# A two-block transformer kernel: constant products ahead of the first slab, a new order for the first head round, branch splits over the last gate slabs, and a few reordered steps

## The chip, the cores and the metric

The kernel runs on one core of one Trainium2 chip. The metric is the device time of one execution in microseconds (us). A core has TensorE (PE, matrix products into PSUM banks), VectorE (DVE), ScalarE (ACT), GpSimd (POOL) and SyncE (SP, which here issues nearly all DMAs). The engines run their own instruction streams in order and meet through semaphores.

## The reference

Two blocks work on x of 512 tokens by 1024 features, all in float32.

```python
# block 1: gated delta rule (8 heads, chunks) and forgetting attention (8 heads)
u = rmsnorm(x, norm_mix_g);  proj = u @ w_in          # q, k, v, z, gates, fq, fk, fv, ff, gate_a, gate_b
qkv = silu(causal_depthwise_conv([gq, gk, gv]))       # then l2norm of q and k, per head
o_a = gated_delta_rule(q, k, v, g, beta);  o_b = forgetting_attention(fq, fk, fv, log_f)
merged = sigmoid(gate_a) * (o_a @ w_proj_gdn) + sigmoid(gate_b) * (o_b @ w_proj_fox)
h = x + merged @ w_out;  x = h + square(relu(rmsnorm(h) @ w_up)) @ w_down
# block 2: retention (4 heads) and sliding-window attention with sinks (16 query, 2 key heads)
ry = silu(rg) * head_group_norm(retention(rotary(rq), rotary(rk), rv));  ay = window_attention(...)
merged = sigmoid(gate_a) * (ry @ w_ret_out) + sigmoid(gate_b) * (ay @ w_attn_out)
x = x + merged @ w_out;  x = x + (silu(h2 @ w_gate) * (h2 @ w_up)) @ w_down
return rmsnorm(x, lnf_g)
```

## The kernel before, in words

**Slabs.** All large weights are cut into 302 slabs of 1024 by 128 (8 tiles of 128x128). SP loads a slab into one of four `slab_raw` buffers. ACT casts it to `slab_hi` (L269), POOL subtracts to get `slab_lo` (L276, two halves), and only then may SP load the slab four places later into that buffer. An activation is split in the same way: ACT writes `u_hi` (L492), DVE writes `u_lo` (L497). One slab is then 24 products on PE: hi by hi (L287), hi by lo activation (L288) and lo by hi (L289) for each of 8 tiles, all into one PSUM bank. PE waits for `slab_lo` before the first product of a slab. DVE takes the finished bank away ("evacuation", eJ for slab J) and multiplies it by the norm row `r_row`.

**Orders.** Every engine walks the same list of tokens. `sJ.T` is tile T of slab J (on ACT and POOL `sJ.0` is the split of slab J+2), `eJ` is the evacuation, and every other token is a step that each engine takes part in or ignores. For block 1, `FIRST` orders head round 0 (7 slabs, and the gate and norm setup `nsq`, `nrow`, `nrc`, `gates0` to `gates4`), `ORDER` the rounds 1 to 7, in which the small steps of the head before are spread between the slabs of the next, and `LAST`, built from `ORDER`, the eight gate slabs ahead. `cvX.W` are the convolution steps on DVE, `thX`/`slX` the tanh on ACT and the silu on DVE, `tq`, `tfq`, `tk`, `tfk` transposes of q and k on PE. `YL` and `XL` are the two products of a level of the triangular inverse (L1518): Y on PE, a copy on ACT, X on PE, then a subtraction and a transpose on DVE, on which the next Y waits. In block 2 `FIRST2`, `ORDER2` and `LAST2` do the same for 10 key/value and first-head slabs, three rounds of 8 slabs and 8 gate slabs. There `sp0` to `sp2` build the retention states on DVE (L1198) from products on PE, `ro` (L937, L939) reads them, `M2` is the scaling of attention probabilities on DVE (L1257 to L1264), `T2`/`T3` transposes of probabilities (L977), `sg` and `bn` DVE steps.

**Start.** SP issues the gains, half of x (1 MB), slab 0, the other half, slab 1, four small tables, `x_tok` (2 MB, for the norm), slabs 2 and 3. One semaphore, `ld_small`, covers the small tables and `x_tok`. PE begins when `slab_lo` of slab 0 is there.

**Between rounds and merge.** After the gate slabs, the outputs of both branches are split (`branch_hi` on ACT L564, `branch_lo` on DVE L577, 16 pairs of tiles each engine). In block 1 these steps are already spread over the last gate slabs (`brK` in `LAST`); in block 2 they all come after the last gate slab.

**End.** The last norm adds squares of 8 tiles (ACT, POOL). PE sums over partitions with a matrix of ones (L517, L519), DVE scales (L533), POOL takes the power (L508), PE spreads it to a row (L525), DVE multiplies the 8 output tiles (L1388), and SP stores each.

Of the kernel before, what the change touches and what calls it, by code (L numbers as in the profile page):

```python
# [26 lines left out]
P = 128  # L27
T = 512
NT = T // P
# [105 lines left out]
def program(nc, dram, out):  # L135
# [23 lines left out]
    with ExitStack() as ctx:  # L159
# [120 lines left out]
        def slab_products(pe, ph, i, j, bank, x_hi, x_lo, ks=range(KT), n_k=KT):  # L280
# [9 lines left out]
            if ks[-1] == n_k - 1:  # L290
# [78 lines left out]
                   s1.1 bs tv T0 bi s1.2 s1.3 S1 s1.4 vp E1 s1.5 s1.6 kpd s1.7 P1 s2.0 Y3 s2.1 s2.2 X3 O0 e1 s2.3  # L369
# [34 lines left out]
        FIRST = [t for t in ORDER if is_slab(t) or is_evac(t) or t in LATE]  # L404
        FIRST.remove("tq")
        FIRST.insert(FIRST.index("tfq"), "tq")
        FIRST.insert(FIRST.index("s0.0") + 1, "nsq")
        FIRST.insert(FIRST.index("s2.3"), "nrow")
        FIRST.insert(FIRST.index("e0"), "nrc")
        FIRST.insert(FIRST.index("s1.2"), "gates0")  # L410
        FIRST.insert(FIRST.index("s1.7"), "gates0t")
        FIRST.insert(FIRST.index("e1") + 1, "gates1")
        FIRST.insert(FIRST.index("e3") + 1, "gates2")
        FIRST.insert(FIRST.index("e4") + 1, "gates3")
        FIRST.insert(FIRST.index("s6.0") + 1, "gates4")
# [94 lines left out]
        def norm_pe(pe, n):  # L510

            pe.wait_ge(sem("norm_sum"), (n - 1) * (KT - 1) + (KT - 2 if n == 4 else KT - 1))
            if n == 4:
                pe.wait_ge(sem("norm_sq"), n * KT + 1)
            for t in range(NT):
                q = slice(t * P, (t + 1) * P)
# [3 lines left out]
            mm.then_inc(sem("norm_ps"), 1)  # L520

        def norm_pe_row(pe, n):
            pe.wait_ge(sem("norm_pool"), n + 1)
            for t in range(NT):
                mm = pe.transpose(bF[:, t * P:(t + 1) * P], r_col[:, t:t + 1].to_broadcast([P, P]), ident[:])  # L525
            mm.then_inc(sem("norm_ps"), 1)

        def norm_dve(dve, n):
            if n == 0:
                dve.wait_ge(sem("norm_sq"), 1)  # L530
            else:
                dve.wait_ge(sem("norm_ps"), 2 * n)
            dve.tensor_scalar(ms_col[:], ms_col[:] if n == 0 else bF[:, 0:NT], 1.0 / D, EPS, ALU.mult, ALU.add)\  # L533
                .then_inc(sem("norm_ms"), 1)
# [254 lines left out]
        def mlp_dve(dve):  # L789
            def part(i):  # L790
                for j in range(16):
# [67 lines left out]
                    s3.0 e2 sp0 lg3 s3.1 s3.2 sp1 E3 s3.3 s3.4 M2 sp2 s3.5 s3.6 s3.7 ro tg M3 s4.0 T2 e3 s4.1 bn  # L859
                    s4.2 T3 sg s4.3 s4.4 s4.5 O1 nm s4.6 s4.7 ev1 s5.0 ty s5.1 s5.2 yo s5.3 e4 s5.4 swan rbn s5.5 s5.6  # L860
# [11 lines left out]
        for tok, place in zip(("rbn", "swqn", "swkn", "rqn", "rkn", "swan", "ran"),  # L872
                              ("s5.6", "s6.2", "s6.4", "s6.6", "s7.2", "s8.2", "s8.6")):
# [15 lines left out]
        def ret_pe(pe, tiles, transposes):  # L889
            def per_round(tokens, ph, i, c):  # L890
# [59 lines left out]
                def logits(a_):  # L950
# [7 lines left out]
                    pe.sem_inc(sem("logits_begun"), 1)  # L958
# [23 lines left out]
                def outs(a_):  # L982
# [5 lines left out]
                    pe.sem_inc(sem("outs_begun"), 1)  # L988
# [18 lines left out]
        def ret_act(act):  # L1007
# [7 lines left out]
            def per_round(tokens, ph, i, c):  # L1015
# [66 lines left out]
                def ev(a_):  # L1082
# [5 lines left out]
                          "swkn": lambda: swrn(1), "swa1": swa1, "swan": swan}  # L1088
                for a_ in range(2):
                    stages[f"ev{a_}"] = lambda a_=a_: ev(a_)  # L1090
# [8 lines left out]
        def ret_dve(dve, step):  # L1099
# [17 lines left out]
            def per_round(tokens, ph, i, c):  # L1117
# [154 lines left out]
                for u in range(4):  # L1272
                    stages[f"lg{u}"] = lambda u=u: logits(u)
                    stages[f"M{u}"] = lambda u=u: sums(u)
                if c is None:
# [25 lines left out]

        FFN_PARTS = [(ph_ffn, 0, 8), (ph_ffn, 1, 8), (ph_ffn_end, 0, FF2_TILES - 16)]
# [33 lines left out]
        def ffn_act(act):  # L1336
# [19 lines left out]
            square(KT - 1)  # L1356

        def ffn_dve(dve):
# [28 lines left out]
            for m in range(KT):  # L1387
# [3 lines left out]
        def ffn_pool(pool):  # L1391
# [6 lines left out]
            norm_pool_scale(pool, 4)  # L1398

# [27 lines left out]
        def after_heads_dve(dve, step):  # L1427
# [4 lines left out]
            for k in range(KT):  # L1432
                branch_lo(dve, 1, k)
# [900 lines left out]
```

## Time and profile before

| | us |
|---|---|
| three runs | 1964.81, 1964.97, 1965.12 |
| profiled execution, its own time | 1964.55 |
| its span, first to last instruction | 1962.8 |
| PE busy | 1918.7 |
| DVE, POOL, ACT busy | 939.1, 914.5, 686.3 |

Times inside the trace count from the start of the span, and 1.75 us lie around it. A PE row of a product is longer than the distance to the next one, because products overlap in the array; what a product costs is the distance between starts.

### The profile page before, as it was taken

To read this page: it belongs to the slowest core of one execution; us is meant where nothing else is said; L and a number is where in the kernel's file an instruction comes from. 1 tells how busy PE (TensorE), PEld (TensorE's weight loads), DVE (VectorE), ACT (ScalarE), POOL (GpSimd) and SP (SyncE) were. 2 spreads that over 40 slices of the span, in tenths; PEclk is the share of its full clock that TensorE was granted. 3 is DMA by queue.
4 is the path that set the end of the run, shared out by engine and by line. 5 is a ranking of instruction groups with operands and counts; after the bars stand their busy time and mean duration, and the time that the engine had idled before them with its cause. 6 is when DMAs were issued, how large, how long until landed. Compare 5 with 4: busy or idle time off the path is not lost.

```text
span 1962.8 us, 27161 instructions
## 1 busy us (share of the span) xinstructions
PE 1918.7 (98%) x9893; PEld 1569.9 (80%) x9893; DVE 939.1 (48%) x1642; ACT 686.3 (35%) x1379; POOL 914.5 (47%) x695
## 2 busy tenths in 40 slices
PE   7899999999999999999999999999999999999997
PEld 5788878888788888888888877778788888888886
DVE  4777777777652222121212467778522235244143
ACT  4344333443332234232324445545422332222122
POOL 3444345443444465444445533434345556555455
PEclk9999999999999999999999999999999999999999
DMA  5122111221223342333332322112133323323232
GB/s 195 56 86 85 64 64 43 85 85 64 65 77 106 129 143 97 97 97 97 96 97 97 118 76 75 64 64 65 64 141 104 100 86 97 108 86 101 92 97 75
DMA packets 53046, 178.55 MB, mean 91 GB/s; under 512 B 6704, under 2 KB 7664, under 8 KB 52720
## 3 DMA queue, kind: packets, MB, share of 16 engines
q1 hardware_dynamic: 52480, 174.95, 27.1%
q10 hardware_dynamic: 496, 2.65, 0.4%
q8 instruction: 46, 0.75, 0.2%
q14 instruction: 24, 0.20, 0.0%
HBM read 173.35 MB, written 4.23 MB: 90 GB/s over the span
## 4 chain that ended last, share of the span: by engine, by line
PE 88%; DVE 8%; ACT 2%; issue 2%; DMA 0%; POOL 0%; DVEq 0%; POOLq 0%; ACTq 0%; SPq 0%
PE bank L287 26%; PE bank L289 25%; PE bank L288 25%; PE bank L1507 2%; PE bank L1501 2%; PE bank L1518 1%; PE bank L1697 1%; PE bank L1684 1%; PE bank L992 1%; DVE att_neg_max L1251 1%; ACT slab_hi L269 1%; PE bank L963 1%; PE bank L977 0%; DVE block_rows L2076 0%; PE bank L937 0%
## 5 line engine op out<-in xcount | busy, mean ns | idle before, releaser
L276 POOL TENSOR_TENSOR slab_lo<-slab_raw,slab_hi 128x512 fp32r<-128x512 f32 x604 | 818.2, 1380 | 954.8 <-ACT slab_hi L269 954.7
L287 PE MATMUL bank<-u_hi,slab_hi 128*128 128x512 f32 x1584 | 653.8, 413 | 14.1 <-POOL slab_lo L276 13.5
L289 PE MATMUL bank<-u_hi,slab_lo 128*128 128x512 f32 x1584 | 620.3, 392 | 0.0
L288 PE MATMUL bank<-u_lo,slab_hi 128*128 128x512 f32 x1584 | 618.6, 391 | 0.0
L269 ACT CAST slab_hi<-slab_raw 128x1024 fp32r<-128x1024 f32 x302 | 313.9, 1045 | 219.6 <-PE bank L289 218.5
L287 PEld LDWEIGHTS bank<-u_hi,slab_hi 128*128 128x128 f32 x1584 | 298.6, 189 | 76.4 <-issue 18.2
L289 PEld LDWEIGHTS bank<-u_hi,slab_lo 128*128 128x128 f32 x1584 | 297.9, 188 | 64.1
L288 PEld LDWEIGHTS bank<-u_lo,slab_hi 128*128 128x128 f32 x1584 | 299.1, 189 | 55.2 <-issue 1.9
L287 PE MATMUL bank<-hidden_hi,slab_hi 128*128 128x512 f32 x432 | 168.4, 390 | 0.3
L288 PE MATMUL bank<-hidden_lo,slab_hi 128*128 128x512 f32 x432 | 168.1, 389 | 0.0
L289 PE MATMUL bank<-hidden_hi,slab_lo 128*128 128x512 f32 x432 | 168.1, 389 | 0.0
L503 DVE TENSOR_TENSOR residual<-residual,bank 128x512 f32<-128x512 f32 x48 | 33.0, 688 | 200.6 <-PE bank L289 200.6
L287 PEld LDWEIGHTS bank<-hidden_hi,slab_hi 128*128 128x128 f32 x432 | 81.1, 188 | 18.4 <-DVE residual L1383 1.6
L288 PEld LDWEIGHTS bank<-hidden_lo,slab_hi 128*128 128x128 f32 x432 | 81.1, 188 | 16.8
L289 PEld LDWEIGHTS bank<-hidden_hi,slab_lo 128*128 128x128 f32 x432 | 81.1, 188 | 16.7
L670 DVE SCALAR_TENSOR_TENSOR mtmp<-mtmp,bank 128x512 f32<-128x512 f32 x32 | 22.0, 688 | 129.9 <-PE bank L289 129.7
L1348 ACT ACTIVATE tmp<-tmp 128x512 f32<-128x512 f32 x22 | 13.9, 633 | 176.6 <-DVE tmp L1369 176.6
L801 DVE SCALAR_TENSOR_TENSOR tmp<-bank,r_row 128x512 f32<-128x512 f32 x32 | 22.1, 692 | 85.0 <-PE bank L289 84.9
L1383 DVE TENSOR_TENSOR residual<-residual,bank 128x512 f32<-128x512 f32 x24 | 16.5, 688 | 94.8 <-PE bank L289 94.8
L772 ACT ACTIVATE tmp<-tmp 128x512 f32<-128x512 f32 x32 | 20.2, 632 | 109.0 <-DVE tmp L801 109.0
L486 POOL TENSOR_TENSOR sq_sum<-sq_sum,mtmp 128x512 f32<-128x512 f32 x27 | 35.0, 1298 | 47.4 <-ACT mtmp L477 47.4
L287 PE MATMUL bank<-branch_a_hi,slab_hi 128*128 128x512 f32 x128 | 51.4, 401 | 3.0 <-DVE branch_a_lo L577 3.0
(353 smaller groups left out, 2581.0 us busy)
## 6 DMA issues: line engine op xcount, KB each, us to landing
slab_raw<-slabs SPq DMA_DIRECT2D x302, 512.0 KB, 3.5
g_and_cum_rows<-row_store SPq DMA_DIRECT2D x7, 512.0 KB, 6.4
residual<-x_t SPq DMA_DIRECT2D x2, 1024.0 KB, 7.0
x_tok<-x SPq DMA_DIRECT2D x1, 2048.0 KB, 12.9
residual<-x_t SPq DMA_DIRECT2D x1, 2048.0 KB, 9.1
residual_store<-residual SPq DMA_DIRECT2D x1, 2048.0 KB, 9.8
residual<-residual_store ACTq DMA_DIRECT2D x1, 2048.0 KB, 9.1
out_t<-residual SPq DMA_DIRECT2D x8, 256.0 KB, 2.1
```

What stands on the lines that cost most here:

```text
L269: act.copy(w_hi[s][:], raw[s][:]).then_inc(s_hi, 1)
L276: ins = pool.tensor_tensor(w_lo[s][:, ks, :], raw[s][:, ks, :], w_hi[s][:, ks, :].bitcast(F32), ALU.subtract)
L287: pe.matmul(bank, w_hi[s][:, k, :], x_hi[:, k, :], start=first, stop=False)
L288: pe.matmul(bank, w_hi[s][:, k, :], x_lo[:, k, :], start=False, stop=False)
L289: mm = pe.matmul(bank, w_lo[s][:, k, :], x_hi[:, k, :], start=False, stop=last)
L486: pool.tensor_tensor(sq_sum[:], sq_sum[:], mtmp[m % 2][:], ALU.add).then_inc(sem("norm_sum"), 1)
L503: ins = dve.tensor_tensor(h_res[:, m, :], h_res[:, m, :], bank[:], ALU.add)
L670: dve.scalar_tensor_tensor(out=merge_g[j][:], in0=merge_g[j][:], scalar=1.0, in1=branch_banks(m, ahead)[j][:], op0=ALU.add, op1=ALU.mult). ...
L772: act.activation(tmp[2 + t % 2][:], tmp[t % 2][:], ACT.Square).then_inc(sem("hid_sq"), 1)
L801: dve.scalar_tensor_tensor(out=tmp[j % 2][:], in0=bank_slab[j % 2][:], scalar=0.0, in1=r_row[:], op0=ALU.max, op1=ALU.mult).then_inc(sem(" ...
L1501: mm = pe.matmul(out_[:, c], lhs[:, c], rhs[:, c], start=start, stop=stop)
L1507: mm = pe.transpose(out_[:, c], in_[:, c], ident[:])
```

## The change

Seven parts:

1. **Constant products.** PE begins with 34 products of the constant matrix `ones` with itself (128x128, f32) into a bank that nothing reads, as soon as DVE has set `ones`.
2. **Loads.** x comes in three pieces (2, 2 and 4 tiles), slab 0 right behind the first, then slabs 1 and 2 and the small tables, `x_tok` under a semaphore of its own, then slab 3.
3. **First two slabs.** DVE instead of POOL makes `slab_lo` of slab 0, between `u_lo` tiles 1 and 2. POOL waits until all of `u_lo` is done. PE takes slab 0 by an explicit list, high parts first, and of slab 1 first all products with `slab_hi`, then the eight with `slab_lo`.
4. **Order of round 0.** `FIRST` is written out: evacuations and convolutions start earlier relative to the slabs, and the second half of `gates1` becomes `gates1b`.
5. **Orders.** `X3` moves behind `O0 e1 s2.3`; in block 2 `sp2` before `M2`, `sg` and `s4.3` before `T3`, `kva` from s2.4 to s2.7, `swan` and `ran` from slab 8 to slab 7.
6. **Branch splits.** In block 2 `br0` to `br7` go into `LAST2`, from s5.4 to s7.3.
7. **Last norm.** PE sums the seven added tiles into one bank early and the last tile alone into another; tiles 6 and 7 are scaled on ACT in advance and multiplied by the row on POOL, DVE keeps six.

Some semaphores are merged or renamed. The core of the diff:

```diff
-s1.1 bs tv T0 bi s1.2 ... s2.1 s2.2 X3 O0 e1 s2.3
+s1.1 bs tv T0 bi s1.2 ... s2.1 s2.2 O0 e1 s2.3 X3
...
-        FIRST = [t for t in ORDER if is_slab(t) or is_evac(t) or t in LATE]
...
+        FIRST = """s0.0 nsq s0.1 s0.2 s0.3 s0.4 s0.5 s0.6 s0.7 s1.0 nrc s1.1 gates0 s1.2 s1.3 s1.4 s1.5 s1.6 s1.7 s2.0
+                   nrow e0 s2.1 cv0.0 gates0t s2.2 cv0.1 s2.3 cv0.2 s2.4 cv0.3 s2.5 e1 th0 s2.6 gates1 s2.7 cv1.0 s3.0
+                   cv1.1 s3.1 e2 s3.2 sl0 s3.3 gates1b s3.4 cv1.2 s3.5 cv1.3 s3.6 tq s3.7 th1 s4.0 s4.1 gates2 s4.2 e3
+                   s4.3 cv2.0 s4.4 cv2.1 s4.5 cv2.2 s4.6 cv2.3 gates3 s4.7 tfq sl1 th2 s5.0 s5.1 e4 s5.2 sl2 s5.3 gates4
+                   s5.4 tk s5.5 s5.6 tfk s5.7 s6.0 e5 s6.1 cola s6.2 colh s6.3 s6.4 s6.5 s6.6 s6.7""".split()
...
-                mm = pe.matmul(bF[:, t:t + 1], sq_sum[:, q], ones[:, 0:1], start=True, stop=n != 4)
-                if n == 4:
-                    mm = pe.matmul(bF[:, t:t + 1], mtmp[1][:, q], ones[:, 0:1], start=False, stop=True)
+            if n == 4:
+                pe.wait_ge(sem("norm_sq"), n * KT + 1)
+                for t in range(NT):
+                    mm = pe.matmul(bE[:, t:t + 1], mtmp[1][:, t * P:(t + 1) * P], ones[:, 0:1], start=True, stop=True)
...
-            if rnd == 1:
-                for k in range(KT):
-                    branch_hi(act, 1, k)
...
-                    s3.0 e2 sp0 lg3 s3.1 s3.2 sp1 E3 s3.3 s3.4 M2 sp2 s3.5 s3.6 s3.7 ro tg M3 s4.0 T2 e3 s4.1 bn
-                    s4.2 T3 sg s4.3 s4.4 s4.5 O1 nm
+                    s3.0 e2 sp0 lg3 s3.1 s3.2 sp1 E3 s3.3 s3.4 sp2 M2 s3.5 s3.6 s3.7 ro tg M3 s4.0 T2 e3 s4.1 bn
+                    s4.2 sg s4.3 T3 s4.4 s4.5 O1 nm
...
+        for k, place in enumerate(("s5.4", "s5.6", "s6.0", "s6.2", "s6.4", "s6.6", "s7.1", "s7.3")):
+            LAST2.insert(LAST2.index(place), f"br{k}")
...
-        FIRST2.insert(FIRST2.index("s2.4"), "kva")
+        FIRST2.insert(FIRST2.index("s2.7"), "kva")
...
-                              ("s5.6", "s6.2", "s6.4", "s6.6", "s7.2", "s8.2", "s8.6")):
+                              ("s5.6", "s6.2", "s6.4", "s6.6", "s7.2", "s7.3", "s7.7")):
...
+        POOL_TILES, DVE_TILES = (6, 7), (0, 1, 2, 3, 4, 5)
...
+            for m in POOL_TILES:
+                act.activation(h_res[:, m, :], h_res[:, m, :], ACT.Copy, scale=gains[:, 4, m:m + 1])
+            act.wait_ge(sem("norm_ps"), 11)
+            act.copy(r_row[:], bE[:]).then_inc(sem("act_step"), 1)
...
+            for m in POOL_TILES:
+                pool.tensor_tensor(h_res[:, m, :], h_res[:, m, :], r_row[:], ALU.mult).then_inc(sem("pool_result"), 1)
...
-            for k in range(KT):
-                branch_lo(dve, 1, k)
...
+        WARM = 34
+        FIRST_SLAB = [[("hh", 0)], [("hh", 1), ("hl", 0)], [("hl", 1), ("hh", 2)],
+                      [("hh", 3), ("lh", 0), ("lh", 1), ("lh", 2), ("lh", 3)],
+                      [("hl", 2), ("hl", 3), ("hh", 4)], [("hh", 5), ("lh", 4), ("lh", 5), ("hl", 4)],
+                      [("hl", 5), ("hh", 6)], [("hh", 7), ("lh", 6), ("lh", 7), ("hl", 6), ("hl", 7)]]
+        X_PIECES = ((0, 2, "ld_x_first"), (2, 4, "ld_x_second"), (4, 8, "ld_x"))
...
+            for m in (0, 1, 2, 3, 6, 4, 5, 7):
...
+            def second_slab(t, bank):
+                if t == 0:
+                    pe.wait_ge(s_hi, 2)
+                pe.matmul(bank[:], w_hi[1][:, t, :], u_hi[:, t, :], start=t == 0, stop=False)
+                pe.matmul(bank[:], w_hi[1][:, t, :], u_lo[:, t, :], start=False, stop=False)
+                if t == KT - 1:
+                    pe.wait_ge(s_lo, 2)
+                    for k in range(KT):
+                        mm = pe.matmul(bank[:], w_lo[1][:, k, :], u_hi[:, k, :], start=False, stop=k == KT - 1)
+                    mm.then_inc(s_used, 1)
+
+            pe.wait_ge(sem("setup_dve"), 1)
+            for n in range(WARM):
+                pe.matmul(bA[:, 0:P], ones[:], ones[:], start=True, stop=True)
...
+                if k == 1:
+                    dve.wait_ge(s_hi, 1)
+                    dve.tensor_tensor(w_lo[0][:], raw[0][:], w_hi[0][:].bitcast(F32), ALU.subtract).then_inc(s_lo, 1)
...
-            for j in range(LEAD):
-                split_lo(pool, ph_heads, 0, j)
+            pool.wait_ge(s_lo, 1)
+            pool.wait_ge(sem("u_lo"), KT)
+            split_lo(pool, ph_heads, 0, 1)
```

## Rows read from the trace of the kernel before

**Rows 1.** The page, part 1: busy time (share of the span), instructions.
```profile
PE 1918.7 (98%) x9893; PEld 1569.9 (80%) x9893; DVE 939.1 (48%) x1642; ACT 686.3 (35%) x1379; POOL 914.5 (47%) x695
```
**Rows 2.** Waits of PE, whole span: who waited for whom: us, times, longest.
```profile
PE bank L287 <- POOL slab_lo L276: 13.5, 1, 13.5
PE bank L937 <- DVE ret_state L1198: 5.5, 4, 1.4
PE bank L287 <- DVE branch_a_lo L577: 3.0, 2, 2.7
PE bank L1518 <- ACT inv_and_prod L1813: 2.8, 8, 0.6
PE bank L1507 <- DVE ck L1983: 2.0, 1, 2.0
PE bank L1507 <- DVE cq L1983: 1.7, 1, 1.7
...
PE bank L977 <- ACT att_probs_t L1079: 0.9, 4, 0.3
PE bank L1507 <- DVE raw_fq L1904: 0.7, 1, 0.7
PE bank L963 <- DVE att_q L1115: 0.6, 1, 0.6
PE bank L1507 <- DVE ret_k L1150: 0.5, 1, 0.5
```
**Rows 3.** Timeline of the start: start us, us, what, xcount [idle before <-releaser].
```profile
1.11 0.27 DVE L1877 MEMSET inv_t_full<- 64x256 f32 x1
...
6.69 1.28 ACT L492 ACT_TABLE_LOAD   x1 [6.69 <-DMA residual<-x_t]
...
8.74 1.41 DVE L497 SCALAR_TENSOR_TENSOR u_lo<-residual,gains,u_hi 128x512 fp32r<-128x512 f32 x2 [7.35 <-ACT u_hi L492]
...
10.16 3.78 ACT L492 ACTIVATE u_hi<-residual,gains 128x512 fp32r<-128x512 f32 x6
...
10.91 7.68 DVE L497 SCALAR_TENSOR_TENSOR u_lo<-residual,gains,u_hi 128x512 fp32r<-128x512 f32 x6 [0.76 <-ACT u_hi L492]
```
**Rows 4.** Chain that ended last, 13 to 75 us: start us, us, what.
```profile
18.52 0.43 PE bank L289
...
19.51 0.23 PE bank L289
...
69.07 0.44 PE bank L1507 x4
...
72.73 0.89 PE bank L1501 x8
```
**Rows 5.** Windows: PE, PEld, DVE, ACT, POOL busy, granted clock, DMA share, GB/s.
```profile
4.00:6.00 2.00, 0.00 (x0) 0.00 (x0) 0.00 (x0) 0.00 (x0) 0.00 (x0) 1.00 1.04 404
```
**Rows 6.** Timeline of head round 2, the step X3 on DVE, then Y4 on PE.
```profile
150.03 0.45 DVE L2095 STREAM_TRANSPOSE inv_and_prod<-inv_t 128x256 f32<-128x256 f32 x1
...
151.86 0.68 PE L1518 MATMUL bank<-inv_and_prod,a_levels 64*64 64x64 f32 x16
```
**Rows 7.** Window in the branch splits of block 2 (columns as in rows 5).
```profile
1410.00:1411.00 1.00, 1.00 (x4) 0.81 (x3) 1.00 (x3) 1.00 (x3) 0.00 (x0) 0.50 0.00 0
```
**Rows 8.** Chain that ended last, 1405 to 1418 us.
```profile
1405.92 0.24 PE bank L289
...
1408.83 0.60 DVE branch_b_lo L577
...
1417.31 0.50 PE bank L287
```
**Rows 9.** Timeline of the end.
```profile
1950.79 0.35 PE L517 MATMUL bank<-ones,sq_sum 128*128 128x1 f32 x2 [1.53 <-ACT mtmp L477]
...
1952.75 0.16 DVE L533 TENSOR_SCALAR ms_col<-bank 128x4 f32<-128x4 f32 x1 [2.76 <-PE bank L519]
...
1954.95 5.36 DVE L1388 SCALAR_TENSOR_TENSOR residual<-residual,gains,bank 128x512 f32<-128x512 f32 x8 [2.04 <-PE bank L525]
```

More of the change, by code:

```diff
@@ L1274, in per_round @@
                     stages[f"M{u}"] = lambda u=u: sums(u)
+                for k in range(KT):
+                    stages[f"br{k}"] = lambda k=k: branch_lo(dve, 1, k)
                 if c is None:
@@ L1386, in ffn_dve @@
             dve.wait_ge(sem("norm_ps"), 9)
-            for m in range(KT):
+            dve.scalar_tensor_tensor(out=ms_col[:], in0=bE[:, 0:NT], scalar=1.0 / D, in1=ms_col[:], op0=ALU.mult,
+                                     op1=ALU.add).then_inc(sem("norm_ms"), 1)
+            dve.wait_ge(sem("norm_ps"), 10)
+            for m in DVE_TILES:
                 dve.scalar_tensor_tensor(out=h_res[:, m, :], in0=h_res[:, m, :], scalar=gains[:, 4, m:m + 1],
@@ L1452, in _ @@
                 sp.dma_start(dst, src).then_inc(sem(name), 16)
-            sp.dma_start(x_tok[:], dram["x"].rearrange("(n p) d -> p n d", p=P)).then_inc(sem("ld_small"), 16)
-            for j in range(2, ph_heads.n):
+            sp.dma_start(x_tok[:], dram["x"].rearrange("(n p) d -> p n d", p=P)).then_inc(sem("ld_x_tok"), 16)
+            first_slab(3)
+            for j in range(SLOTS, ph_heads.n):
                 s = ph_heads.slot(j)
@@ L1519, in quads, with first_slab @@
                 return mm
+            def first_slab(t, bank):
+                for kind, k in FIRST_SLAB[t]:
+                    first, last = (kind, k) == ("hh", 0), (kind, k) == ("hl", KT - 1)
+                    if kind == "hh":
+                        if k == 0:
+                            pe.wait_ge(s_hi, 1)
+                        pe.wait_ge(sem("u_hi"), k + 1)
+                        mm = pe.matmul(bank[:], w_hi[0][:, k, :], u_hi[:, k, :], start=first, stop=False)
+                    elif kind == "hl":
+                        pe.wait_ge(sem("u_lo"), k + 1)
+                        mm = pe.matmul(bank[:], w_hi[0][:, k, :], u_lo[:, k, :], start=False, stop=last)
+                    else:
+                        if k == 0:
+                            pe.wait_ge(s_lo, 1)
+                        mm = pe.matmul(bank[:], w_lo[0][:, k, :], u_hi[:, k, :], start=False, stop=False)
+                mm_last = mm
+                if t == KT - 1:
+                    mm_last.then_inc(s_used, 1)
+            def second_slab(t, bank):
[3 more added lines that the diff above has]
+                pe.matmul(bank[:], w_hi[1][:, t, :], u_lo[:, t, :], start=False, stop=False)
+                if t == KT - 1:
+                    pe.wait_ge(s_lo, 2)
+                    for k in range(KT):
+                        mm = pe.matmul(bank[:], w_lo[1][:, k, :], u_hi[:, k, :], start=False, stop=k == KT - 1)
[3 more added lines that the diff above has]
+                pe.matmul(bA[:, 0:P], ones[:], ones[:], start=True, stop=True)
             def head_round(tokens, i, c):
@@ L1533, in slab @@
                     if isinstance(i, int) and i == 0 and j == 0:
[L1534 removed]
+                        first_slab(t, bank)
+                        return
+                    if isinstance(i, int) and i == 0 and j == 1:
+                        second_slab(t, bank)
+                        return
                     slab_products(pe, ph, ph_i, j, bank[:], u_hi, u_lo, ks=(t,))
```

104 lines of the change are left out of this document (54 added, 50 removed).

## The prediction

> **What bounds the kernel now.** I began with the page. TensorE is busy for 98% of the span [rows 1], so no other engine can be the bound as a whole, and the change takes no products away (it adds some). What is left to win is time in which TensorE does nothing or runs at the lower clock, and that is found in two views: the list of waits with TensorE as the waiting engine [rows 2], and the timeline at the few places that this list names. The reader is to see in [rows 2] that one wait, 13.5 us at the very start, is nearly half of the sum, and that the rest is small waits that come back once a round. The list leaves one kind of loss out: products that run but slowly. It shows in the distance between starts. The last product of the slow stretch at the start takes 0.43 us to the next, one of the fast stretch 0.23 [rows 4]; that is 1.2 against 2.4 GHz for 512 columns. The column of the granted clock does not show it at the start (it reads 1.00 there), while it reads 0.50 in the second slow stretch, in the branch splits of block 2 [rows 7].
>
> **Part 1 to 4, the start, by sums.** Before, TensorE starts at 13.5 us, when POOL has finished the low part of slab 0, and runs 13 products at the low clock, until 18.9. The first step of round 1 starts at 69.07 [rows 4]. The 55.6 us between hold 13 x 0.20 = 2.6 us of low clock and 2.0 + 1.7 + 0.7 = 4.4 us of waits for the convolved q and k and for an evacuation [rows 2]. So the work of round 0 itself is 55.6 - 2.6 - 4.4 = 48.6 us, and the new start of round 1 is the time at which real products begin, plus 48.6, plus new waits.
>
> When do real products begin? DVE has set the constants at 1.4 us [rows 3], and then come 34 products in f32 of 128 columns. Four such products stand in the trace as 8 instructions in 0.89 us [rows 4], so one instruction costs 0.111 us at full clock and 34 products are 68 of them. No row has this shape at the low clock; between 0.111 (the weight load hidden) and twice that, I take 0.222, because the 512-column products do double. The low clock lasted 5.4 us after the idle start. So 5.4 / 0.222 = 24 instructions at the low clock, 44 x 0.111 = 4.9 us at the full one, and the end is 1.4 + 5.4 + 4.9 = 11.7 us. If the clock rose at once it would be 1.4 + 68 x 0.111 = 9.0; if not at all during these products, 1.4 + 68 x 0.222 = 16.5.
>
> Are the data there at 11.7? The first MB of x had landed at 6.7 [rows 3]; at 404 GB/s [rows 5] half a MB less is 1.3 us less, 5.4. ACT loads its table (1.28), makes two tiles of `u_hi` at 0.63, which is what six of them in 3.78 us cost [rows 3], and casts slab 0 (1024 columns, an estimate of 1.1 from the same row): 9.1. DVE then makes `slab_lo` of slab 0; no row has DVE at 1024 columns, so it lies between one split of 512 columns, 0.6 [rows 8], and two with a start-up, 1.4; I take 1.3, since twice the columns are what it does: 10.4. After that come six tiles of `u_lo`. Before they took 7.68 us, 1.28 each, while POOL was splitting slabs; the first two, with POOL idle, took 1.41 together [rows 3]. POOL now waits until they are done, so I count 0.67 each, 4.0, and the last one stands at 14.4 us. ACT's last `u_hi` does not set it: six more at 0.63 from 9.1 and the rest of x, another 1.5 MB at 404 GB/s behind slab 0, end near 13.1. TensorE, from 11.7, reaches the last low activation as its 24th product, at 11.7 + 23 x 0.227 = 16.9, so nothing waits, and the margin is 2.5 us. Slab 1 asks for its high part at 17.1 (ready near 14) and its low part only after gates0 (24 products, 5.5 us) and the other high products, near 26; POOL makes it from 14.4 to 17.3. The delay of POOL costs nothing for that reason.
>
> What is late next is the setup of the norm. `x_tok` goes ahead of slab 3 only, so it is the sixth MB; five more at 404 GB/s behind the first are 12.4 us, with the small tables near 20. Four squares on ACT of 1024 columns (an estimate, 1.1 each) and the power on POOL, and r is there near 26. `nrow` stands at 11.7 + 17.5 = 29.2 on TensorE. From there DVE has a chain: row, e0, four steps of q's convolution, e1, six small gate steps, and so on. Written out at 0.7 us a step it gives silu of q at 38.4 (TensorE wants it at 39), the gate table at 41.2 (wanted at 41.6), e3 at 45.9 (wanted at 46.6), silu of k at 49.4 (wanted at 50.4). Each margin is positive and under 1.2 us, so I take no new wait, and up to 2 us for the range. The second half of the gate steps needs two table loads on ACT, and between the two halves DVE now works at convolutions. Sum: 11.7 + 48.6 = 60.3 against 69.07, a gain of **8.8 us**.
>
> **Part 5, orders.** `X3` waits 2.8 us in 8 rounds for a copy on ACT that is queued behind the cast of a slab [rows 2]. Behind `O0` and one tile of a slab (0.2 + 0.7 us) the copy is long done: gain 2.8. The price can be on the next step: before, DVE ends the transpose for `Y4` at 150.48 and `Y4` starts at 151.86 [rows 6], 1.4 us of room; X3 runs 0.6 us later net of the wait, and e1 on DVE, which it lets pass, uses the wait, so 0.4 or more is left. I count nothing. In block 2, `ro` waits 5.5 us in four rounds for the last state [rows 2]. DVE writes that state behind the four operations of `M2`, and the releaser named in the row is this write. With `sp2` ahead of `M2` it comes before TensorE wants it; its product stands three tiles earlier (2.0 us). `M2` moves back by one short operation, which `T2` does not feel, as it stands behind all 14 instructions of `ro`. Gain 5.5, and if only half of the wait were `M2`, 2.8. `T3` waited 0.9 in all for copies on ACT and gets one more tile, 0.7 us each: gain 0.9. `kva` three tiles later clears 0.5, and `swan` and `ran` a slab earlier clear 0.6 at the first logits [rows 2]. ACT then waits for the evacuation of slab 6 with the swaps, and behind it are only casts which wait for slab 8 anyway. Sum: **10.3 us**.
>
> **Part 6, branch splits.** The last gate product ends at 1406.16 in the chain, the product on the last low tile of branch a starts at 1417.31 [rows 8] and the slab ends with it, 3 products later, at 1418.3. Unhindered it would end 24 x 0.227 = 5.4 after 1406.0, at 1411.4. So 6.9 us hang on the splits: 2.7 in the wait, the rest in the low clock [rows 7] and in splits of DVE at 0.60 each, two for each tile [rows 8]. After the change DVE has, from s5.4 to the end of slab 7 (20 tiles, 13.6 us), 16 x 0.60 = 9.6 us of splits and two evacuations of 1.2: 12.0. They fit, and TensorE is hindered only if e5 is late for slab 7, which begins 5.4 before 1406.0, at 1400.6. Ahead of e5 stand br0 to br2, 3.6 us from about 1393.8, so e5 ends near 1398.6. What is queued behind the splits on ACT is the cast of slab 8: it waits for six copies, ends near 1397.5, and POOL has the low part at 1400 for a use at 1406. SP's load of slab 12 waits for that low part, and is wanted 20 us later. Gain **6.9 us**.
>
> POOL works at two slabs meanwhile. The rows show that this matters: `u_lo` at 1.28 us beside POOL and 0.7 without [rows 3], the splits at 0.60 beside an idle POOL [rows 8]. The page "SBUF — State Buffer" of the Trainium skill (section Who interferes with whom) says that a VectorE instruction with two SBUF inputs and a GpSimd one that reads SBUF exclude each other for the whole instruction; [rows 3] agrees. By that rule these two slabs block DVE for another 5.1 us, the last split comes at 1411 instead of 1406, and the gain is 6.4 instead of 6.9.
>
> **Part 7, the end.** 16 instructions at 0.11 us lie between the last square and DVE's scaling at 1952.75 [rows 9]. Eight of them move ahead of the last square: 0.9. DVE's 8 tiles at 0.67 [rows 9] become 6: 1.3. POOL's two begin behind four more instructions on PE and a copy on ACT (1.1 us) and have until DVE's sixth, so POOL may take 1.4 us a tile where DVE takes 0.67; I take it that they just end. Stores go out one by one, of 256 KB, 0.65 us each at the rate of [rows 5], and that takes back 0.1. Gain **2.1 us**.
>
> **Sum.** 8.8 + 10.3 + 6.9 + 2.1 = 28.1 us. The profiled execution took 1964.55, so 1936.45; the median of the runs is 0.4 above it, and I predict **1936.8 us**.
>
> **Rivals.** (A) The forecast.
> (B) *The clock does not rise during the constant products*, because they load weights as long as they multiply. Real products begin at 16.5 and the first 13 run at the low clock: 4.8 + 2.6 = 7.4 us less gain, 1944.2. For it: no row of this shape starts from the low clock. Against: rounds with many small products stay at 0.23.
> (C) *Small waits come back elsewhere.* The gains of part 5 and of the conv chain leave margins of 0.3 to 1 us. If half of part 5 is lost at the next step (5.2 us), 1942.0. For it: DVE, the second busiest engine [rows 1], makes nearly all that these steps wait for. Against: each of these waits had nothing of the same kind behind it in [rows 2].
> (D) *The splits move the wait to slab 7*, which doesn't do what it says. If the six splits ahead of e5 run at 1.28 instead of 0.60, e5 ends 4.1 us later, 2.2 after slab 7 wants it: 1939.0.
> (E) *Slower: the low clock stays.* If the constant products and then round 0 itself run at the low clock, each us of work costs one more. Real products begin at 16.5 (4.8 later), and the gain of 28.1 is used up when 23 of the 48.6 us of round 0 have run at half speed; with all of it, 1936.8 + 4.8 + 48.6 = 1990. Against: the low stretch at the start ended after 5.4 us of steady work, though of products of another shape.
>
> **Chances.** A 0.64, B 0.09, C 0.12, D 0.04, E 0.03 (0.01 of it stopping within 0.2% of before), and 0.08 for a larger gain than A: the gaps that TensorE's queue leaves around each cleared wait, and constant products that end at 9 to 10, together up to 4 us, 1932.8. Range 1932.8 to 1942.0: the low end is that case, the high end is C, and it leaves out B and E, 0.12. Less than 0.2% either way, 3.9 us, is about what a measurement of this kernel can't tell from no change; only E and an error of over 20 us reach it. So faster 0.97 (all but E), same 0.01, slower 0.02.
>
> **What would show it.** In the changed trace: real products from 11.7 us at 0.23 apart; the last `u_lo` near 14.4; the first step of round 1 near 60; no wait of TensorE for the copy before X3 nor for the state; the first merge product right behind the last gate product, with the clock at 1.00; DVE's last output tile 2.2 us sooner after the last square. The prediction is wrong if constant products last to 16, if round 0 has waits of over 2 us for DVE, or if a wait appears at slab 7 of the last gate round.

## The result, and the profile after

The changed kernel takes **1939.64 us** (median of four runs, 1939.38 to 1940.0), against 1964.89 for the kernel before in the same comparison; the ratio is 0.9875, 95% interval [0.9864, 0.9887]. The forecast was 1936.8 with a range of 1932.8 to 1942.0. The profiled execution took 1939.53, with a span of 1937.7; its own gain in span is 1962.8 - 1937.7 = 25.1 us, where the sum of the terms said 28.1.

The page after, part 1, answers to [rows 1]:

```profile
PE 1920.6 (99%) x9965; PEld 1576.2 (81%) x9965; DVE 949.7 (49%) x1642; ACT 688.3 (36%) x1382; POOL 917.7 (47%) x695
```

The waits of TensorE after answer to [rows 2] (who waited for whom: us, times, longest):

```profile
PE bank L1757 <- DVE k_dec L2110: 3.1, 8, 1.3
PE bank L1575 <- DVE inv_t_full L1937: 1.4, 1, 1.4
PE bank L519 <- POOL r_col L501: 1.4, 1, 1.4
PE bank L287 <- DVE branch_a_lo L573: 1.2, 1, 1.2
PE bank L1529 <- DVE raw_fq L1967: 0.9, 1, 0.9
...
PE bank L1633 <- DVE table L2007: 0.5, 1, 0.5
```

The wait of 13.5 us for `slab_lo` is gone, and so are those for `ret_state`, for the convolved q and k, and for the copy at `X3`. The first line was 0.2 us in one place before. What it has gained is almost exactly the wait of 2.8 us at `X3` that went. L1757 is `O0`, the step that `X3` was moved behind.

**Where the 25.1 us came from.** The same step stands in both traces, so the difference of its start times tells how much had been gained by then. Read at the borders of the stages it gives:

| stage | forecast | measured |
|---|---|---|
| start, to the first step of round 1 | 8.8 | 8.6 |
| rounds of block 1 (`X3`) | 2.8 | -0.3 |
| to the rounds of block 2 (`kva`, `swan`, `ran`) | 1.1 | 1.9 |
| four rounds of block 2 (`sp2`, `T3`) | 6.4 | 8.5 |
| merge of block 2 (splits) | 6.9 | 5.3 |
| last norm and stores | 2.1 | 1.2 |
| sum | 28.1 | 25.1 (rounded terms: 25.2) |

The sum is off by 3.0, with errors of both signs in it: 2.9 us too little in the rounds of block 2 and on the way to them, 5.8 us too much elsewhere. That the total came so near is in part luck.

The start. The chain of the changed kernel, start us and us (`x68` are the constant products):

```profile
1.43 9.36 PE bank L1575 x68
10.79 0.46 PE bank L1550 x2
...
28.61 0.70 DVE r_row L534
...
46.06 1.13 DVE block_rows L2029
47.21 0.70 DVE raw_fq L1967
47.96 0.66 PE bank L1529 x4
...
60.49 0.44 PE bank L1529 x4
```

Real products begin at 10.8 instead of the forecast 11.7, and round 1 at 60.49 against 69.07 in [rows 4]. Between the two the chain leaves TensorE and runs over DVE, with two table loads of ACT (1.28 us each) in it, from the row of the norm at 28.6 to `raw_fq`.

The merge. The timeline of DVE ahead of it (start us, us, what):

```profile
1387.81 0.68 DVE L1144 TENSOR_TENSOR residual<-bank,r_row 128x512 f32<-128x512 f32 x1
1388.52 0.80 DVE L1146 TENSOR_SCALAR residual<-residual,round_bias 128x512 f32<-128x512 f32 x1
1389.25 1.77 DVE L573 TENSOR_TENSOR branch_a_lo<-branch_a,branch_a_hi 128x512 fp32r<-128x512 f32 x1
1390.95 1.77 DVE L573 TENSOR_TENSOR branch_b_lo<-branch_b,branch_b_hi 128x512 fp32r<-128x512 f32 x1
1392.65 0.68 DVE L573 TENSOR_TENSOR branch_a_lo<-branch_a,branch_a_hi 128x512 fp32r<-128x512 f32 x1
1393.25 0.68 DVE L573 TENSOR_TENSOR branch_b_lo<-branch_b,branch_b_hi 128x512 fp32r<-128x512 f32 x1
```

A split takes 1.77 us or 0.68. POOL's low parts of slabs run from 1382.4 to 1392.2 with a pause of 0.27 us, and every split that starts in that stretch is a long one. TensorE takes the last tile of branch a at 1393.38, after a wait of 1.15 us.

The end. The timeline of the last norm answers to [rows 9]:

```profile
1926.79 1.05 PE L512 MATMUL bank<-ones,mtmp 128*128 128x1 f32 x8 [0.66 <-ACT mtmp L470]
1927.95 0.16 DVE L1390 SCALAR_TENSOR_TENSOR ms_col<-bank,ms_col 128x4 f32<-128x4 f32 x1 [1.62 <-PE bank L512]
...
1930.00 4.04 DVE L1394 SCALAR_TENSOR_TENSOR residual<-residual,gains,bank 128x512 f32<-128x512 f32 x6 [1.89 <-PE bank L519]
...
1931.51 2.49 POOL L1407 TENSOR_TENSOR residual<-residual,r_row 128x512 f32<-128x512 f32 x2 [2.31 <-ACT r_row L1359]
```

DVE ends at 1934.04, 1.3 us sooner after its first tile than before, as forecast; but the span ends at 1937.7. From DVE's first tile to the end it was 7.85 us before (1954.95 to 1962.8) and is 7.7 now.

### The profile page after: what moved, and what is told of

Its sections match the earlier page's. It is cut to its first block, busy times and chain, and to the rows that moved or that the text cites. A ratio compares the mean times of both kernels' runs of the same rounds, so it can differ in the third digit from the quotient of the medians.

```text
span 1937.7 us, 27308 instructions
## 1 busy us (share of the span) xinstructions
PE 1920.6 (99%) x9965; PEld 1576.2 (81%) x9965; DVE 949.7 (49%) x1642; ACT 688.3 (36%) x1382; POOL 917.7 (47%) x695
## 4 chain that ended last, share of the span: by engine, by line
PE 92%; DVE 6%; issue 1%; ACT 0%; DVEq 0%; POOL 0%
PE bank L287 27%; PE bank L289 26%; PE bank L288 26%; PE bank L1529 2%; PE bank L1523 2%; PE bank L1540 1%; PE bank L1757 1%; PE bank L1744 1%; PE bank L986 1%; PE bank L957 1%; PE bank L971 1%; PE bank L1575 0%; DVE block_rows L2147 0%; DVE branch_a_lo L573 0%; DVE branch_b_lo L573 0%
## 5 line engine op out<-in xcount | busy, mean ns | idle before, releaser
L287 PE MATMUL bank<-u_hi,slab_hi 128*128 128x512 f32 x1568 | 646.3, 412 | 0.2
L289 PE MATMUL bank<-u_hi,slab_lo 128*128 128x512 f32 x1568 | 613.0, 391 | 0.0
L288 PE MATMUL bank<-u_lo,slab_hi 128*128 128x512 f32 x1568 | 611.5, 390 | 0.0
L1347 ACT ACTIVATE tmp<-tmp 128x512 f32<-128x512 f32 x22 | 13.9, 632 | 176.6 <-DVE tmp L1372 176.6
L479 POOL TENSOR_TENSOR sq_sum<-sq_sum,mtmp 128x512 f32<-128x512 f32 x27 | 35.1, 1299 | 47.4 <-ACT mtmp L470 47.4
L485 ACT ACTIVATE u_hi<-residual,gains 128x512 fp32r<-128x512 f32 x32 | 22.7, 723 | 89.8 <-DVE residual L496 85.0
```

Source lines behind the costliest of these rows:

```text
L287: pe.matmul(bank, w_hi[s][:, k, :], x_hi[:, k, :], start=first, stop=False)
L288: pe.matmul(bank, w_hi[s][:, k, :], x_lo[:, k, :], start=False, stop=False)
L289: mm = pe.matmul(bank, w_lo[s][:, k, :], x_hi[:, k, :], start=False, stop=last)
L479: pool.tensor_tensor(sq_sum[:], sq_sum[:], mtmp[m % 2][:], ALU.add).then_inc(sem("norm_sum"), 1)
L485: act.activation(u_hi[:, m, :], h_res[:, m, :], ACT.Copy, scale=gains[:, n, m:m + 1])\
```

## The experiments

Each edits the changed kernel; an edit not shown is told in its expectation. All times are medians of four runs. They come from several comparisons, and the kernel before, run beside each, had medians from 1963.26 to 1964.89 us. So a difference of about 1.5 us or less between medians of two comparisons shows little by itself, and what is said of such gains rests on the distances in the traces.

**1. Where `X3`'s gain went.** Two kernels, `X3` back in its old place, and `O0` one tile later:

```diff
-s2.1 s2.2 O0 e1 s2.3 X3
+s2.1 s2.2 X3 O0 e1 s2.3     (a2)
+s2.1 s2.2 s2.3 O0 e1 X3     (a1)
```

> The changed kernel with X3 back in its old place (X3 O0 e1 s2.3). Theory 1, the move exchanged one wait for another of the same size: the wait for ACT's copy at X3 (2.8 us) returns, the wait at O0 (3.1 us) goes, and the time is 1939.6 within 0.7 us. Theory 2, the prediction's sum: the move gains 2.8 us and something else ate the rest, so without it the time is 1942.4.

Measured: **1939.33 us**, the changed kernel's time. The waits of TensorE with `X3` back:

```profile
PE bank L1540 <- ACT inv_and_prod L1873: 2.5, 8, 0.4
```

The wait for `k_dec` is not in its list. The move by itself is worth nothing.

> The changed kernel, with O0 one slab tile later (s2.3 O0 e1 X3 for O0 e1 s2.3 X3), so that X3 stays where the change put it. Theory 1, the wait only moved: in the changed kernel TensorE waits 3.1 us in 8 rounds at O0 for DVE's k_dec, each wait 0.25 to 0.4 us, and the tile of 0.68 us covers them; each listed wait costs some 0.15 us more than its row says, so the time falls from 1939.6 by 3 to 4.5 us, to 1935 to 1936.6. Theory 2, DVE's chain behind X3 (subtraction, transpose, then Y4) has no room left: the wait comes up at Y4 or T1 instead, and the time stays within 1 us of 1939.6.

Measured: **1936.59 us** (1935.77 to 1937.83), 3 us faster than the changed kernel. From 80 to 500 us TensorE has no wait in the list at all, where the changed kernel has this:

```profile
PE bank L1757 <- DVE k_dec L2110: 1.5, 6, 0.3
```

Each round is 0.51 us shorter, for 0.25 of listed wait; the other 0.26 stands beside it. Only the last head keeps some:

```profile
PE bank L1757 <- DVE k_dec L2110: 0.6, 1, 0.6
PE bank L1529 <- DVE probs L2227: 0.4, 1, 0.4
```

So the room behind `X3` that the forecast doubted was there (Y4 waits for nothing), and the step that failed was one it never looked at: `O0`, which took `X3`'s place in the order. In round 2 of the changed kernel TensorE could begin `O0` at 139.13, DVE's `k_dec`, for which it waits, ends at 139.40, and `O0` begins at 139.55.

**2. The merge: DVE beside POOL.**

> The changed kernel with the branch splits of block 2 behind the last gate slab again, on ACT and DVE, as before the change. By the distances between the two traces the move gained 5.3 us, so 1944.9; the prediction's term was 6.9, so 1946.5 by that; if the extra work that the splits bring to DVE and POOL in the gate round costs elsewhere, less than 5 us.

Measured: **1944.96 us**, 5.3 more than the changed kernel. The term is 5.3, not 6.9. The distances in the traces give 5.3 against this kernel and against the kernel before alike, although TensorE's clock is low for 3.4 us of the splits here and for 6.8 there. DVE makes a pair of splits in 1.20 us, and TensorE takes a tile in 0.7 us at the full clock and 1.28 at the low one. When the clock rises it catches up, and in both kernels it takes the last tile of branch a 0.05 or 0.06 us after DVE has made it. So the splits set the pace, and the low clock, to which the prediction gave a part of the price, cost nothing here.

> The changed kernel with nearly all of POOL's work during the last gate round of block 2 left out: of each of the eight low parts made in that round (slabs 2 to 9 counted from its start) only 16 columns of one tile are computed. Theory 1, DVE's branch splits take 1.77 us each where POOL subtracts at the same time and 0.6 to 0.7 where it does not: all 16 now take 0.6 to 0.7, DVE is done some 8 us earlier, the wait before the last tile of branch a goes, and the time falls by 1.3 to 1.6 us to 1938.0 to 1938.3. Theory 2, the long splits have another cause (ACT's writes, DMAs): they stay at 1.77 us and the time stays at 1939.6.

```diff
+            if ph is ph_gates2:
+                pool.tensor_tensor(w_lo[s][:, 0, 0:16], raw[s][:, 0, 0:16], w_hi[s][:, 0, 0:16].bitcast(F32),
+                                   ALU.subtract).then_inc(s_lo, 1)
+                return
```

Measured: **1938.16 us**, 1.5 less. Groups of DVE from 1374 to 1394 us by form (busy us, mean ns), first the changed kernel, then this one:

```profile
L573 DVE TENSOR_TENSOR branch_a_lo<-branch_a,branch_a_hi 128x512 fp32r<-128x512 f32 x8 | 8.8, 1095 | 0.7 <-ACT branch_a_hi L560 0.7
L573 DVE TENSOR_TENSOR branch_b_lo<-branch_b,branch_b_hi 128x512 fp32r<-128x512 f32 x8 | 8.7, 1093 | 0.0
```

```profile
L577 DVE TENSOR_TENSOR branch_b_lo<-branch_b,branch_b_hi 128x512 fp32r<-128x512 f32 x8 | 6.6, 821 | 0.0
L577 DVE TENSOR_TENSOR branch_a_lo<-branch_a,branch_a_hi 128x512 fp32r<-128x512 f32 x8 | 5.5, 684 | 0.7 <-ACT branch_a_hi L564 0.7
```

All eight splits of branch a now take 0.68 us; of branch b only the last, which falls beside the slabs that POOL still does in full, is long. The wait at the merge is gone (1.5 us there by the distances), and POOL is shown as the cause. The page "SBUF — State Buffer" of the Trainium skill (section Who interferes with whom) says that a VectorE instruction with two SBUF inputs contends with a GpSimd instruction that reads SBUF. This case agrees, at 1.77 against 0.68 us.

> The changed kernel with the evacuation e6 of the last gate round behind the last branch split br7 (three tiles later), so that DVE makes the splits 1.5 us earlier. Theory 1, DVE is short of time before the merge because its splits take 1.77 us beside POOL: each us given back there counts, and of the 1.6 us that TensorE loses at the last tile of branch a 1.2 to 1.6 come back: 1938.0 to 1938.4. Theory 2, DVE would then run its next instructions more often against POOL's and gain nothing: 1939.6 within 0.4.

Measured: **1939.41 us**, no gain in the time, as theory 2 had it; by the distances in the trace 0.4 us come back at the merge, where theory 1 put 1.2 to 1.6. DVE ahead of the merge in this kernel:

```profile
1387.97 1.78 DVE L573 TENSOR_TENSOR branch_a_lo<-branch_a,branch_a_hi 128x512 fp32r<-128x512 f32 x1
1389.67 1.77 DVE L573 TENSOR_TENSOR branch_b_lo<-branch_b,branch_b_hi 128x512 fp32r<-128x512 f32 x1
1391.36 1.77 DVE L573 TENSOR_TENSOR branch_a_lo<-branch_a,branch_a_hi 128x512 fp32r<-128x512 f32 x1
```

The evacuation e6 costs 0.68 and 0.80 us beside a busy POOL, and 0.68 and 0.49 alone. Taken out of POOL's time, it makes room for one more split, which POOL stretches to 1.77. Time given back to DVE is worth little as long as POOL holds it to one split per 1.7 us.

> The changed kernel with another order of the branch splits on ACT and DVE, in both blocks: all eight tiles of branch a first, then the eight of branch b (before: a0, b0, a1, b1 and so on). The merge takes a's eight tiles in its first 5.4 us and b's in the next 5.4. Theory 1, the wait at the merge comes from the order only, since b's tiles are made before they are needed: a's last tile stands some 6 us earlier, b's last one stays at 1393.9 and is wanted at about 1396.5, so the wait of 1.2 us and some 0.3 beside it go: 1938.0 to 1938.4. Theory 2: DVE as a whole is too late for the merge, and the wait moves to branch b or to the evacuation e7: 1939.6 within 0.4.

```diff
-            for hi, br in ((a_hi, br_a), (b_hi, br_b)):
-                act.copy(hi[:, k, :], br[:, k, :]).then_inc(sem("br_hi"), 1)
+            hi, br = ((a_hi, br_a), (b_hi, br_b))[k // 4]
+            for q in (2 * k % KT, 2 * k % KT + 1):
+                act.copy(hi[:, q, :], br[:, q, :]).then_inc(sem("br_hi"), 1)
```

(`branch_lo` and TensorE's counts follow in the same way.) Measured: **1938.65 us** (1937.88 to 1938.92), 1.0 less by the medians and 1.4 at the merge by the distances in the trace. DVE in this kernel:

```profile
1379.65 2.38 DVE L576 TENSOR_TENSOR branch_a_lo<-branch_a,branch_a_hi 128x512 fp32r<-128x512 f32 x2
1381.96 5.78 DVE L576 TENSOR_TENSOR branch_b_lo<-branch_b,branch_b_hi 128x512 fp32r<-128x512 f32 x4
```

The last tile of branch a is done at 1382.0 instead of 1393.3, those of branch b as late as before, and TensorE waits for neither. DVE was not short of time; it made things in another order than TensorE takes them. By the traces it is the same gain that silencing POOL brought.

**3. The start: what the constant products do.**

> The changed kernel without the 34 constant products. Real products can then begin when slab_hi and u_hi are there, near 7.1 us in the changed trace, at the low clock for some 3.5 us as the constant products had it. Theory 1: slab 0 can't end before the last u_lo (13.93 us) and the small tables (15.9 us) and x_tok (21.0 us) arrive as before, so the row of the norm and DVE's chain behind it set the start of round 1; it stays at 60.5 us and the time at 1939.6 within 0.5 us. Theory 2, the constant products are what makes the start fast: the waits between the first products hold the clock low into slabs 0 and 1, round 1 starts 2 to 5 us later, and the time is 1941.5 to 1944.5.

Measured: **1939.59 us** (1938.93 to 1941.25): no difference. TensorE in this kernel:

```profile
7.50 1.19 PE L1550 MATMUL bank<-u_hi,slab_hi 128*128 128x512 f32 x2 [7.50 <-ACT slab_hi L269]
```

It starts 3.0 us sooner (its row stands at 10.55 in the changed kernel), at the low clock (4 products from 7.50 to 9.34), begins slab 1 at 14.9 instead of 16.1, and then waits 1.5 us for `w_gates_lo`. The step ahead of round 1 stands at 60.43, and at 60.33 with the constant products.

The eleven profiles that have both the constant products and the new order of round 0 say the same without an edit. Their 68 instructions take from 9.36 to 10.78 us, and the first product of the gates begins between 17.13 and 18.42; but the step ahead of round 1 stands between 59.95 and 60.77 in all but one (c1, below), and not later where the gates are. The kernel with the slowest ones (a4, 10.78) has it at 60.54.

The traces also show what it does follow: the landing of `x_tok`. ACT's squares of `x_tok` begin when it lands and end between 24.58 us (c3) and 25.98 (c1), and from there to the step ahead of round 1 it is 35.1 to 35.6 us in all eleven, and 35.4 without the constant products. The end of the squares in the changed kernel and in c1:

```profile
25.06 0.19 ACT L1910 ACTIVATION_READ_ACCUMULATOR x_tok<-x_tok 128x1 f32 x1
```

```profile
25.80 0.18 ACT L1910 ACTIVATION_READ_ACCUMULATOR x_tok<-x_tok 128x1 f32 x1
```

A likely link is POOL, whose low parts of slabs follow the power of the norm: in the changed kernel they end at 31.52, and DVE's first step of q's convolution beside them takes 1.46 us and ends at 31.81; in c3 they end at 30.85 and the same step, behind them, takes 0.49. No run moved that load or these slabs, so this is not shown.

Inside the 68 the clock explains the spread. Windows of 1 us of the changed kernel and of c1, where they took 10.48 (the busy time and count of each engine, granted clock, DMA share, GB/s):

```profile
3.40:4.40 1.00, 1.00 (x7) 1.00 1.07 416
4.40:5.40 1.00, 1.00 (x10) 1.00 1.07 434
5.40:6.40 1.00, 1.00 (x12) 1.00 0.98 383
```

```profile
4.40:5.40 1.00, 1.00 (x6) 1.00 1.05 430
5.40:6.40 1.00, 1.00 (x7) 1.00 0.99 385
6.40:7.40 1.00, 1.00 (x9) 1.00 1.06 404
```

With 6 or 7 of them in 1 us the clock is low (0.213 us between starts), with 12 it is full (0.111), and the windows with 9 and 10 hold the change; the column of the granted clock reads 1.00 throughout. The change comes at 4.6 us in the one and 7.0 in the other, and that is where each trace's own record of the clock begins: the 1.00 ahead of it stands for no record.

> The changed kernel with the order of head round 0 derived as before the change (gates1b directly behind gates1); the constant products, loads and first two slabs stay. The prediction put 4.4 us of the start on the waits for the convolved q and k and an evacuation, which the order removes, while the changed order has 1.4 us of waits of its own. Theory 1: those waits come back at about their old size, less 1.4, with some 0.15 us each beside their rows: 3 to 3.6 us slower, 1942.6 to 1943.2. Theory 2: real products begin 3 us sooner than before the change while the row of the norm comes no sooner in proportion, so DVE is later against TensorE than it was, the waits grow beyond their old size, and the time is over 1944.

Measured: **1945.79 us** (1944.47 to 1948.01), 6.2 more. Its waits:

```profile
PE bank L1537 <- DVE ck L2062: 2.0, 1, 2.0
PE bank L1537 <- DVE cq L2062: 1.7, 1, 1.7
...
PE bank L1634 <- ACT gates_row L1813: 1.3, 1, 1.3
```

They are the old ones in their old size, not larger, so theory 2 has the right number for the wrong reason: listed waits of 5.7 us less the 1.4 of the changed kernel, and 0.16 for each of the two more, are 4.6 us, and some 2 us are left (round 1 starts 6.8 us later in the trace). Most of them are in the clock (window: us, then PE, PEld, DVE, ACT, POOL busy, granted clock, DMA share, GB/s):

```profile
52.00:56.00 4.00, 2.48 (x10) 1.95 (x11) 3.24 (x6) 3.83 (x26) 0.00 (x0) 0.75 0.61 248
56.00:60.00 4.00, 4.00 (x18) 3.26 (x17) 0.79 (x2) 2.70 (x13) 2.54 (x2) 0.82 0.03 8
```

Behind the waits, in which TensorE was busy for 2.76 of 4 us and then 2.48 of 4, products stand 0.43 us apart until the clock rises at 57.4. It fell at 54.0, and 3.4 us at half the clock are 1.7 us. So 6 of the 8.6 us of the start hang on the order. What the other loads and the first two slabs bring alone was not tried.

> The changed kernel with two steps of head round 0 later: gates2 behind s4.2 instead of ahead of it, and tfq behind s5.1 instead of ahead of s5.0. Theory 1, these are the only places of round 0 at which DVE is late, and each stands alone: the waits of 0.5 us (table) and 0.9 us (raw_fq) go with the 0.15 us that each costs beside its row, and round 1 starts 1.4 to 1.7 us sooner: 1938.0 to 1938.3. Theory 2, DVE's chain is late as a whole: TensorE comes earlier to the transposes of k (tk) and waits there, and less than 0.6 us is gained.

Measured: **1940.3 us** (1939.55 to 1940.68), no gain. The wait for `raw_fq` shrinks to 0.2 us, and a new one appears:

```profile
PE bank L1529 <- DVE ck L2054: 1.0, 1, 1.0
```

DVE is late as a whole, theory 2. Round 1 starts at 61.19 here, the latest of the eleven. The constant products were slow (10.48 us), but they are not the cause: `x_tok` landed 0.7 us later than in the changed kernel, and from the end of its squares it is 35.2 us as elsewhere. Against the changed kernel in the same measure (35.1) the two moved steps brought nothing.

**4. Rounds of block 2.**

> The changed kernel with the order of the steps in the rounds of block 2 as before: M2 ahead of sp2, T3 ahead of sg and s4.3. Theory 1, from the distances between the traces: the two reorders gain 1.55 and 0.41 us in each of four rounds, 7.9 in all, more than their listed waits (1.38 and 0.22), because a wait's row starts at the end of the last product's row and that end lies some 0.16 us behind the point at which the next product would have begun: 1947.4. Theory 2, the prediction's sum by listed waits: 6.4, so 1946.0.

Measured: **1948.8 us**, but 1947.27 to 1949.66, wider than the other kernels. The trace is sharper. Its waits are those of [rows 2] again:

```profile
PE bank L931 <- DVE ret_state L1194: 5.5, 4, 1.4
...
PE bank L971 <- ACT att_probs_t L1073: 0.9, 4, 0.3
```

But by the distances to the changed kernel each `ro`, with 1.38 us in the list, costs 1.55 at its first product and 0.1 more in its first four (1.13 us long instead of 1.02), and each `T3`, with 0.22, costs 0.44. That is 8.2 us for four rounds and not 6.4.

**5. The end.**

> The changed kernel with all eight output tiles on DVE again and stored in order; the early sum of seven tiles stays. Theory 1, the stores set the end: eight of 256 KB at some 403 GB/s are 5.2 us behind the first tile, as fast as DVE makes a tile (0.67 us), so DVE's two tiles on POOL bought nothing: within 0.3 us of 1939.6. Theory 2, the prediction's term: two tiles less on DVE are worth 1.3 us, so 1940.9.

Measured: **1940.24 us** (1940.06 to 1940.58), 0.6 more, between the two theories. The DMAs and the timeline decide: from DVE's first tile to the end it is 7.8 us here, 7.7 in the changed kernel. The rest, 0.5 us, lies ahead of DVE, where the eight transposes took 1.97 us instead of 1.55, and that is the clock: it falls at 1929.28 here, before the first of them, and at 1929.73 in the changed kernel, behind the fourth. So theory 1 has the mechanism, and most of what the two profiles differ by is the clock and not the edit. The stores from 1925 to 1938 us of the changed kernel, in 40 slices:

```profile
DMA  1000000000000000000069999999999999994000
GB/s 50 0 0 0 0 0 0 0 0 0 0 0 25 0 0 0 0 0 0 0 239 410 372 410 403 403 397 403 403 410 403 410 403 410 403 403 170 0 0 0
```

From the first store on, the DMAs are busy without a gap, at some 403 GB/s.

**6. Both edits that gained.**

> The changed kernel with both edits that gained alone: O0 one slab tile later, and the branch splits with all of branch a first. They touch different stages (rounds of block 1, and the merges), so theory 1: they add. By the distances in their traces 4.1 and 1.6 us, 1933.9; by their medians 3.0 and 1.0, 1935.6; so 1933.9 to 1935.6. Theory 2: the merge of block 1 splits in the other order too, and with block 1 running sooner something waits there: over 1936.6, no better than O0 alone.

Measured: **1934.93 us** (1934.68 to 1935.77), ratio to the kernel before 0.9853 [0.9836, 0.9869]. It lies in the range of theory 1: they add. All its runs lie below all of the changed kernel's, by 4.7 us in the median; it is the fastest of the series.

## Why the prediction came out as it did

**Start, 8.8 forecast, 8.6 measured: right in size, by a mechanism of less weight than the text gave it.** The sum went through the time at which real products begin (11.7), plus 48.6 of work. They began at 10.8, and round 1 could have begun at 59.4 by that sum; it began 1.1 later, because DVE's chain brought waits of 0.5 and 0.9 us. Its parts up to the row of the norm held: last `u_lo` at 13.9 (14.4 forecast), the row at 28.1 on TensorE (29.2). What failed is "I take no new wait": `raw_fq` stands at 47.9 where the text put 45.9. What the chain had too short is the way to `block_rows`, and this in a chain whose margins were all said to be under 1.2:

```profile
44.73 1.03 ACT L269 CAST slab_hi<-slab_raw 128x1024 fp32r<-128x1024 f32 x1
...
45.80 0.21 ACT L1819 ACTIVATE table<-table 128x32 f32<-128x32 f32 x1
...
46.06 1.12 DVE L2029 COPY block_rows<-level_mask 128x32 f32<-128x32 f32 x1 [1.08 <-issue]
```

DVE stands idle for 1.08 us because its code waits for two small steps of ACT, of which the last is shown, and these are queued behind the cast of a slab. Then `block_rows` takes 1.12 us. In the kernel before there was 0.43 us of idle, with no cast in the way, and 0.19 for the step. POOL is at a low part from 45.84 on; whether that stretches the step was not tried. Part 1 was read as the pacemaker and is worth nothing here (1939.59 without it). With it falls rival B as it was priced: slower constant products, up to 10.78 us, did not move round 1 in any of the eleven profiles. The low clock lasted 3.2 us from the first of them in the changed kernel (1.43 to 4.61) and 6.1 in the slowest (1.44 to 7.58), at 0.213 us from start to start where the text took 0.222; the 5.4 that the text carried over from the start before lies between.

**`X3`, 2.8 forecast, nothing measured.** This is rival C in one place. The step that failed: the price was sought behind `X3`, at `Y4`, and not at the step that moved forward. `O0` comes one `X3` (0.6 us) and its wait sooner, and `k_dec`, for which it waits, ends 0.27 us too late for that (139.40 against 139.13). The text's own sentence, that behind `O0` the copy is long done, was right.

**`sp2` and `T3`, 6.4 forecast, 8.5 measured; `kva`, `swan`, 1.1 and 1.9.** The mechanism was right, the size too small: a listed wait is not its whole price. A product's row lasts 0.39 us, the next one starts after 0.23, and the wait is counted from the end of the row, so it leaves out 0.16. With eight waits in the rounds of block 2 that is 1.3 us, and 0.1 in the products behind each restart is another 0.8: the 2.1 that were missing. At `O0`, too, 0.51 us a round came back for 0.25 in the list.

**Splits, 6.9 forecast, 5.3 measured.** The term took 0.60 us a split from start to start, as beside an idle POOL, for all 16. Six took 1.77 (1.70 from start to start), 6.6 us more than forecast in all, where the sentence on the port said 5.1 and 1411 us for the last split; in the time of the kernel before it came at 1412.5. Since the splits of a and b go in turn, the last tile of a is ready at 1412.0, and TensorE wants it at 1410.7. The error was to leave this out of the sum, as if it were a matter of the rule alone, though [rows 3] had its price. The first merge product did come without a wait, as forecast; the wait sits 21 products later.

**End, 2.1 forecast, 1.2 measured.** The early sums gave 0.8 (1.96 us between square and scaling before, 1.16 after; forecast 0.9). The term that fell is DVE's two tiles, 1.3. The text knew the 0.65 us a store takes and counted 0.1 against it; but eight stores in a row (5.2 us) begin behind the first tile, not the last, and before the change they took as long as DVE's eight tiles to within some 0.1 us. So two tiles less on DVE left the stores as the longer leg.

**Rivals.** D and E did not show: slab 7 of the last gate round has no wait and round 0 ran at the full clock, though c2 shows how near it was: with 3.7 us of waits for the convolutions the clock fell for 3.4 us there, as it had not in the kernel before with waits of the same size.

## What to carry to other kernels

When a step is moved back, look at the one that moves forward in its place: its inputs and its bank must be ready sooner by the same time. Price a removed wait with what its row leaves out (here 0.16 us, and some 0.1 in the products behind it), and a DVE instruction with two SBUF inputs at its price beside POOL if POOL works in that stretch. Where several products wait for a series of small steps, make them in the order in which they are taken. Real products that begin sooner gain nothing where another engine's chain sets the pace behind them (here 1939.59 us without the constant products); and ahead of a stream of stores that already runs without a gap, only its first store is worth time.

## What the hardware did that was not expected

The stretch of low clock at the start is not of one length: 68 instructions of 128 columns in f32 took 9.36 to 10.78 us in eleven executions that began them at the same time, 1.43 or 1.44 us, and the low clock ended between 4.61 and 7.58 us. The same subtraction on DVE takes 0.68 us alone and 1.77 beside POOL's, while a step that takes one of its two inputs from a bank keeps its 0.68. The column of the granted clock reads 1.00 in the first stretch only because the trace has no record of the clock ahead of its end; the distance between starts, 0.213 us against 0.111, is the witness there. And a stretch of low clock cost nothing where TensorE waited for another engine's small steps anyway.
